# Four seven-product pairs instead of three in each feed-forward stage, and the first weight sum made by an accumulating DMA

## The chip, the cores and the metric

The kernel runs on one core of a Trainium2 chip. The metric is the device time of one launch in microseconds (us). Before the change the median of three runs is 1888.43 us (1888.31 to 1888.49).

## The reference

x is 256 tokens by 1024, float32. Four layers; each is a half-step SwiGLU feed-forward, an attention (stick-breaking, differential, forgetting, stick-breaking), and another half-step feed-forward, all on RMS-normed input with residual adds; a last RMS norm ends it. So there are eight feed-forward stages, and the change is in these alone:

```python
D_MODEL, SEQ, DEPTH, D_FF = 1024, 256, 4, 2816
def swiglu(x, w_gate, w_up, w_down):
    return (jax.nn.silu(x @ w_gate) * (x @ w_up)) @ w_down
for i in range(DEPTH):
    x = x + 0.5 * swiglu(rms_norm(x, norm_g[i, 0]), ffn_w_gate[i, 0], ffn_w_up[i, 0], ffn_w_down[i, 0])
    ...                       # attention of the layer, residual add
    x = x + 0.5 * swiglu(rms_norm(x, norm_g[i, 2]), ffn_w_gate[i, 1], ffn_w_up[i, 1], ffn_w_down[i, 1])
return rms_norm(x, final_g)
```

## The kernel before

**Products.** A float32 product is made of three TensorE matmuls. Each operand is split into a high part (`_hi`, a rounded copy) and a low part (`_lo`, the rest); `product()` (L1272 to L1274) issues hi·hi, hi·lo and lo·hi.

**Chunks.** Weights arrive as one stream of chunks, each 128 partitions by 2048 float32 (1 MB). SP issues the loads in the order of `LOADS`, into 4 places of `raw` (and 2 of `extra`). In the order of `USES`, ScalarE (ACT) makes `w_hi` (`hi`, L465), VectorE (DVE) makes `w_lo` (`lo`, L765), TensorE (PE) uses both. `w_hi` and `w_lo` are rings of 6 chunks: ACT may make chunk c once PE is done with chunk c-6. `split_to(c)` means: make all chunks up to c.

**A feed-forward stage** has 11 units of 256 hidden columns. A plain unit takes a `top` and a `bottom` chunk (gate and up weights of 256 columns side by side, 512 of the 1024 inputs each), with 24 matmuls of 512 columns for each (2 token blocks x 4 slices x 3), and a `down` chunk (24 matmuls). Hidden values are turned by 4 transposes, then split as `m_hi` (ACT, L488) and `m_lo` (DVE, L829).

**Seven-product pairs.** Units (2,3), (5,6) and (8,9), listed by `SEVEN`, are done in pairs: with two token blocks and two halves of the inputs, the 2x2 block product is made with seven block products instead of eight (the scheme of Strassen and Winograd). The parts are `b11, t1, t2, b21, t3, t4, b22`, each a chunk of its own and 12 matmuls (`quarter`). The four loaded chunks are b11, b12, b21, b22; the parts t1, t3, t2, t4 are sums of weight chunks that DVE makes (`form`, L778 to L789) in place, t1 and t4 in a buffer `SUMS` (the first place of `extra`). Sums of tokens are made once a stage. The products gather in PSUM banks; ACT copies partial results out, DVE adds them (L918), ACT applies silu, DVE multiplies by the up part (gates).

**What sets the order.** It is written by hand: `FFN_ORDER` gives the order of chunks for all engines, and each engine's function (`plain_step`, `pair_step`) puts its other work between them. Each engine works strictly in this order and waits on semaphores. GpSimd (POOL) only makes `r_col`, the factor 1/rms of each token (L435, L436).

Of the kernel before, what the change touches and what calls it, by code (L numbers as in the profile page):

```python
# [14 lines left out]
P = 128  # L15
# [8 lines left out]
SEVEN = 2, 5, 8  # L24
# [12 lines left out]
CONSTS = 6  # L37
IDLE_TURNS = 20
IDLE_BETWEEN = 8
RAW = 4  # L40
DMA_SCRATCH = 8192
# [23 lines left out]
FORMS = "t1", "t3", "t2", "t4"  # L65
PARTS = "b11", "t1", "t2", "b21", "t3", "t4", "b22"
PAIR_ORDER = *PARTS[:5], "down", *PARTS[5:]


def ffn_order():  # L70
    order = []
    for s in range(UNITS):
        if s in SEVEN:
            order += [(what, s - (what == "down")) for what in PAIR_ORDER]
# [6 lines left out]
    return order + [("down", UNITS - 1)]  # L81
# [43 lines left out]
def plan():  # L125
# [4 lines left out]
    for layer, n, c0, att, no in phases():  # L130
        order = ATT_ORDER if att else FFN_ORDER
        for w, (what, j) in enumerate(order, c0):
            p = no * len(SEVEN) + SEVEN.index(j) if what in PARTS else None
            if what in ("t1", "t4"):
                uses.append((what, no, j, SUMS, None))
            elif what == "t2":
                uses.append((what, no, j, *places["b11"]))
            elif what == "b22":
                uses.append((what, no, j, EXTRA, p + 1))
            elif what == "t3":  # L140
                uses.append((what, no, j, *places["b12"]))
            else:
                uses.append((what, no, j, len(users) % RAW, len(users) // RAW + 1))
            for load in ("b12",) if what == "t1" else () if what in FORMS or what == "b22" else (what,):
# [3 lines left out]
                users.append(("form", len(FORMS) * (p + 1)) if load in ("b11", "b21") else  # L148
                             ("lo", c0 + order.index(("t3", j)) + 1) if load == "b12" else ("lo", w + 1))
            if what == "t1":  # L150
                earlier = SEVEN.index(j) - 1
                loads.append(("b22", layer, n % 3, j, EXTRA,
                              ("top", no * len(PLAIN) + 1) if earlier < 0 else
                              ("lo", c0 + order.index(("b22", SEVEN[earlier])) + 1)))
    return uses, loads


USES, LOADS = plan()


def trunk(nc, stream, x_in, gains, consts, lam_in, subln_in, wf_in, bf_in, final_in, out):
    with ExitStack() as ctx:
# [13 lines left out]
        extra = sb("extra", [P, 2, CHUNK])  # L176

# [24 lines left out]
        final_gain = sb("final_gain", [P, D])  # L202
        mean = sb("mean", [P, TB])
        r_col = sb("r_col", [P, TB])
        half_neg = sb("half_neg", [P, TB])
        mean_apart = sb("mean_apart", [P, TB])
# [36 lines left out]
        b22_loaded, form_ready = sem("b22_loaded"), sem("form_ready")  # L243
        token_sums_ready, token_hi_ready, token_lo_ready = (
# [54 lines left out]
        first_part, second_part, first_sum = (scratch[:, i, 0:2 * T] for i in range(3))  # L299
        h_first, h_sb = ([scratch[:, i, tb * COLS:(tb + 1) * COLS] for tb in range(TB)] for i in (0, 3))  # L300
# [55 lines left out]

        def unit_bank(s, tb):
            return work[:, (TB if s == 1 else 0) + tb, :]

        def hidden_bank(s):  # L360
            return work[:, 1 if s == 0 else 3 if s - 1 in SEVEN else 2, :]

        def hidden_source(s):
            return h_first if s == 0 else h_sb
# [4 lines left out]
        def slot_free(eng, c):  # L369
# [14 lines left out]
            elif what in PARTS:  # L384
                eng.wait_ge(part_psum, (no * len(SEVEN) + SEVEN.index(j)) * len(PARTS) + PARTS.index(what) + 1)
# [10 lines left out]
        def _(sp):  # L396
            def load(i):
                place, free = LOADS[i][4:]
                if free is not None:
                    sp.wait_ge({"lo": lo_ready, "form": form_ready, "top": top_used}[free[0]], free[1])  # L400
                sp.dma_start(raw_at(place), stream[i]).then_inc(b22_loaded if place == EXTRA else raw_loaded[place], 16)
# [1390 lines left out]
```

## Time and profile before

| | |
|---|---|
| median of 3 runs | 1888.43 us |
| the profiled execution: time, span | 1888.84 us, 1887.0 us |
| PE busy | 1873.5 us, 99% |
| DVE busy | 1519.5 us, 81% |
| ACT busy | 1072.5 us, 57% |
| POOL busy | 19.9 us, 1% |
| DMA | 350.13 MB, mean 186 GB/s |

The span runs from the first to the last instruction; 1.84 us of the execution lie around it. Matmuls are pipelined, so the mean of one (some 390 ns) is longer than the distance from one start to the next, and PE busy is not PE at its peak. The same holds, less, for DVE and ACT.

### The profile page before, as it was taken

The page shows a single profiled execution, that of the slowest core. Times are in us where ns is not written, and L with a number is a line of the kernel's source. Part 1 is how long each engine was busy: PE and PEld are TensorE (multiplying, and loading weights), DVE is VectorE, ACT ScalarE, POOL GpSimd, SP SyncE. Part 2 cuts the span into 40 slices and gives each one's busy share as a digit, 9 for nine tenths or more (in the row PEclk, how much of TensorE's full clock was granted, in tenths as well). Part 3 has the DMA queues.
Part 4 walks back from the last instruction along what each step waited for, and adds up shares of the span by engine and source line. Part 5 has one row for each costly group of instructions (what it writes and reads, how often), then busy time and mean ns, then how long its engine had stood idle before and what let it go on. Part 6 is the DMA issues. An engine that isn't in the chain of part 4 may idle for free.

```text
span 1887.0 us, 22407 instructions
## 1 busy us (share of the span) xinstructions
PE 1873.5 (99%) x9364; PEld 1585.5 (84%) x9364; DVE 1519.5 (81%) x1287; ACT 1072.5 (57%) x1108; POOL 19.9 (1%) x34
## 2 busy tenths in 40 slices
PE   9999999999999999999999999999999999999998
PEld 8888998888888899788888888988888888998886
DVE  7987568987898778898789875689879886569985
ACT  6655455655565544565556554465556654556653
POOL 0000000000000000100000000000000000000000
PEclk9999999999999999999999999999999999999999
DMA  6456343556254643444625454434563544533542
GB/s 249 201 231 262 139 157 134 201 201 238 99 224 195 248 157 112 156 201 200 250 102 227 196 229 157 176 115 201 201 268 125 224 198 189 183 130 136 228 197 86
DMA packets 50052, 350.13 MB, mean 186 GB/s; under 512 B 6168, under 2 KB 6432, under 8 KB 7968
## 3 DMA queue, kind: packets, MB, share of 16 engines
q1 hardware_dynamic: 49360, 346.54, 47.1%
q10 hardware_dynamic: 592, 2.17, 0.4%
q8 instruction: 74, 1.21, 0.2%
q14 instruction: 26, 0.21, 0.0%
HBM read 347.63 MB, written 1.06 MB: 185 GB/s over the span
## 4 chain that ended last, share of the span: by engine, by line
PE 89%; DVE 7%; ACT 2%; issue 1%; DMA 0%; POOL 0%; POOLq 0%; ACTq 0%; DVEq 0%
PE work L1272 18%; PE work L1274 18%; PE work L1273 18%; PE acc L1272 10%; PE acc L1274 10%; PE acc L1273 10%; DVE w_lo L765 3%; PE work L1430 1%; PE acc L1316 1%; PE work L1474 1%; PE work L1608 1%; ACT w_hi L465 1%; PE work L1574 0%; DMA x<-x_dram 0%; PE work L1578 0%
## 5 line engine op out<-in xcount | busy, mean ns | idle before, releaser
L765 DVE TENSOR_TENSOR w_lo<-raw,w_hi 128x2048 fp32r<-128x2048 f32 x327 | 741.3, 2283 | 33.5 <-ACT w_hi L465 33.4
L465 ACT ACTIVATE w_hi<-raw 128x2048 fp32r<-128x2048 f32 x327 | 613.9, 1908 | 83.7 <-DVE raw L785 60.9
L1272 PE MATMUL work<-w_hi,xg 128*128 128x512 f32 x1040 | 409.6, 394 | 1.0 <-DVE xg L1197 1.0
L1274 PE MATMUL work<-w_hi,xg 128*128 128x512 f32 x1040 | 405.5, 390 | 0.0
L1273 PE MATMUL work<-w_lo,xg 128*128 128x512 f32 x1040 | 405.0, 389 | 0.0
L1272 PE MATMUL acc<-w_hi,m_hi 128*128 128x512 f32 x824 | 325.5, 395 | 0.2
L1274 PE MATMUL acc<-w_hi,m_lo 128*128 128x512 f32 x824 | 321.2, 390 | 0.0
L1273 PE MATMUL acc<-w_lo,m_hi 128*128 128x512 f32 x824 | 320.7, 389 | 0.0
L1274 PEld LDWEIGHTS work<-w_hi,xg 128*128 128x128 f32 x1040 | 195.2, 188 | 41.1
L1272 PEld LDWEIGHTS work<-w_hi,xg 128*128 128x128 f32 x1040 | 195.3, 188 | 40.5 <-issue 1.2
L1273 PEld LDWEIGHTS work<-w_lo,xg 128*128 128x128 f32 x1040 | 195.5, 188 | 38.8
L765 DVE TENSOR_TENSOR w_lo<-extra,w_hi 128x2048 fp32r<-128x2048 f32 x72 | 164.4, 2283 | 34.2 <-ACT w_hi L465 34.2
L1274 PEld LDWEIGHTS acc<-w_hi,m_lo 128*128 128x128 f32 x824 | 154.7, 188 | 32.7
L1272 PEld LDWEIGHTS acc<-w_hi,m_hi 128*128 128x128 f32 x824 | 154.8, 188 | 31.6 <-DVE w_lo L765 1.0
L1273 PEld LDWEIGHTS acc<-w_lo,m_hi 128*128 128x128 f32 x824 | 154.9, 188 | 30.7
L465 ACT ACTIVATE w_hi<-extra 128x2048 fp32r<-128x2048 f32 x72 | 135.2, 1912 | 46.1 <-DVE extra L778 36.7
L1274 PE MATMUL work<-w_hi,wide_r 128*128 128x512 f32 x384 | 149.7, 390 | 0.0
L1272 PE MATMUL work<-xg,w_hi 128*128 128x256 f32 x512 | 148.7, 290 | 0.2
L1273 PE MATMUL work<-xg,w_hi 128*128 128x256 f32 x512 | 144.7, 283 | 0.0
L1274 PE MATMUL work<-xg,w_lo 128*128 128x256 f32 x512 | 144.7, 283 | 0.0
L488 ACT ACTIVATE m_hi<-work 128x512 fp32r<-128x512 f32 x88 | 49.8, 594 | 141.1 <-PE work L1430 114.5
L829 DVE TENSOR_TENSOR m_lo<-work,m_hi 128x512 fp32r<-128x512 f32 x88 | 58.4, 686 | 71.6 <-ACT m_hi L488 71.5
(203 smaller groups left out, 2151.8 us busy)
## 6 DMA issues: line engine op xcount, KB each, us to landing
raw<-stream_dram SPq DMA_DIRECT2D x303, 1024.0 KB, 5.1
extra<-stream_dram SPq DMA_DIRECT2D x24, 1024.0 KB, 7.0
x<-x_dram SPq DMA_DIRECT2D x2, 512.0 KB, 8.4
raw<-stream_dram ACTq DMA_DIRECT2D x2, 512.0 KB, 7.9
scratch<-cum_rows ACTq DMA_DIRECT2D x1, 1024.0 KB, 6.5
cst<-consts_dram SPq DMA_DIRECT2D x1, 832.0 KB, 6.5
out_dram<-x SPq DMA_DIRECT2D x3, 256.0 KB, 2.4
final_gain<-final_gain_dram SPq DMA_DIRECT2D x1, 512.0 KB, 6.4
```

What stands on the lines that cost most here:

```text
L465: nc.scalar.activation(w_hi[:, c % RING, :], raw_at(place), ACT.Copy).then_inc(hi_ready, 1)
L488: nc.scalar.activation(m_hi[:, u % 2 * 2:u % 2 * 2 + 2, :], halves(hidden_bank(s)), ACT.Copy).then_inc(h_hi_ready, 1)
L765: nc.vector.tensor_tensor(w_lo[:, c % RING, :], raw_at(place), w_hi[:, c % RING, :].bitcast(F32), ALU.subtract).then_inc(lo_ready, 1)
L829: nc.vector.tensor_tensor(m_lo[:, u % 2 * 2:u % 2 * 2 + 2, :], halves(hidden_bank(s)), m_hi[:, u % 2 * 2:u % 2 * 2 + 2, :].bitcast(F32), A ...
L1272: nc.tensor.matmul(dst, a_hi, b_hi, start=start, stop=False, skip_group_check=skip)
L1273: nc.tensor.matmul(dst, a_hi, b_lo, start=False, stop=False, skip_group_check=skip)
L1274: return nc.tensor.matmul(dst, a_lo, b_hi, start=False, stop=stop, skip_group_check=skip)
L1316: ins = nc.tensor.transpose(turned(bank)[:, d, :], x_part(bank)[:, d * P:(d + 1) * P], ident)
L1430: ins = nc.tensor.transpose(hidden_bank(s)[:, t * T + tb * P:t * T + (tb + 1) * P], h[:, t * P:(t + 1) * P], ident)
L1474: ins = nc.tensor.transpose(hidden_bank(s)[:, t * T + tb * P:t * T + (tb + 1) * P], hidden_source(s)[tb][:, t * P:(t + 1) * P], ident)
L1608: nc.tensor.matmul(bank, v[:, 0, cols], w[:, 0:T], start=True, stop=True)
```

## The change

1. `SEVEN` becomes `2, 4, 7, 9`: four pairs a stage instead of three. Pairs 4 and 9 come straight behind a pair (`chained`); plain are only units 0, 1 and 6. The last unit, 10, is now half of a pair.
2. t1 is no longer made by DVE. The chunk b11 is loaded a second time, into `SUMS`, and then GpSimd issues a DMA that adds b12 to it from DRAM (`accum_op=ALU.add`). For this the signs change: all weight sums are now plain additions, the token sums S1, S2, S4 have other signs, and two of the four results come out negated, which the factor `r_neg` (-r_col, made by GpSimd) takes up. t4 is now formed in b21's place.
3. In a chained pair the order of parts is another (`pair_order`): b22's product, the fourth sum's of the tokens, goes ahead, and the down projection of the unit before is done in halves (single banks in the last pair), between quarters.
4. `raw` has 5 places instead of 4; `final_gain` lies in `extra` and is loaded at the end; `DMA_SCRATCH` is 4096 instead of 8192.

```diff
-SEVEN = 2, 5, 8
+SEVEN = 2, 4, 7, 9
-RAW = 4
-DMA_SCRATCH = 8192
+RAW = 5
+DMA_SCRATCH = 4096
-FORMS = "t1", "t3", "t2", "t4"
+FORMS = "t3", "t2", "t4"
+def pair_order(s):
+    if chained(s):
+        return [("b11", s), ("t1", s), ("b21", s), ("down", s - 2), ("b22", s), ("t2", s),
+                ("down", s - 1), ("t3", s), ("t4", s)]
+    return [("b11", s), ("t1", s), ("t2", s), ("b21", s), ("t3", s), ("down", s - 1), ("t4", s), ("b22", s)]
...
+            if what == "down" and chained(j + 2):
+                loads.append(("b22", layer, n % 3, j + 2, EXTRA, ("lo", c0 + order.index(("b22", j)) + 1)))
+            if what == "down" and j + 1 in SEVEN[:-1]:
+                loads.append(("b11", layer, n % 3, following(j + 1), SUMS, ("lo", c0 + order.index(("t1", j + 1)) + 1)))
...
+            def first_weight_sums(no):
+                for p in range(no * len(SEVEN), (no + 1) * len(SEVEN)):
+                    pool.wait_ge(sums_loaded, 16 * (p + 1))
+                    pool.dma_start(raw_at(SUMS), stream[ADD_FROM[p]], accum_op=ALU.add).then_inc(t1_added, 16)
...
+                if n % 3 != 1:
+                    pool.wait_ge(r_col_ready, n + 1)
+                    nc.gpsimd.tensor_tensor(r_neg[:], r_col[:], minus[:], ALU.mult).then_inc(r_neg_ready, 1)
+                    first_weight_sums(n // 3 * 2 + n % 3 // 2)
...
-                if what in FORMS:
+                if what == "t1":
+                    act.wait_ge(t1_added, 16 * count)
+                elif what in FORMS:
...
+                    def second_of_chain():
+                        split_to(q + 4)
+                        hidden_lo(s - 1)
+                        gate_11()
+                        split_to(q + 5)
+                        form("t4", q)
+                        split_to(q + 7)
+                        sum_12()
+                        split_to(q + 8)
+                        gate_12()
+                        sum_22()
+                        gate_22()
+                        split_to(q + 9)
+                        gate_21()
+                        split_to(q + 10)
+                        if s == UNITS - 2:
+                            hidden_lo(s)
+                            hidden_lo(s + 1)
...
+                    if chained(s):
...
+                        quarter(chain, block_of(0, 0), at["b11"], True, False)
+                        pair_hidden(s - 2)
...
+                        quarter(3, sum_of(S1), at["t1"], True, False)
...
+                        quarter(seed, block_of(0, 1), at["b21"], False, True)
...
+                        pair_hidden(s - 1)
+                        unit_down(s - 2).then_inc(down_used, 1)
...
+                        quarter(3, sum_of(S4), at["b22"], False, True)
+                        quarter(chain, sum_of(S2), at["t2"], False, False)
+                        before, between = ((0, 1), (2, 3)) if s < UNITS - 2 else ((0,), (1,))
+                        unit_down(s - 1, before)
...
+                        quarter(chain, sum_of(S3), at["t3"], False, False)
+                        ins = unit_down(s - 1, between)
...
+                        quarter(chain, block_of(1, 1), at["t4"], False, True)
+                        if s == UNITS - 2:
+                            unit_down(s - 1, (2,))
+                            pair_hidden(s)
+                            unit_down(s - 1, (3,)).then_inc(down_used, 1)
+                            pair_hidden(s + 1)
+                            unit_down(s).then_inc(down_used, 1)
```

How instructions move, on three places. On VectorE, in the second half of a pair: before, from the gate of the first block (L927) on; L918 is a sum of partial results, L765 a `w_lo`, L869 and L935 gates, L778 the next pair's t1, L829 an `m_lo`.

```order
L927 SCALAR_TENSOR_TENSOR scratch<-work,r_col,scratch 128x256 [waits pair_silu_ready]
L918 TENSOR_TENSOR scratch<-work,scratch 128x512 [waits part_psum,part_copied]
L765 TENSOR_TENSOR w_lo<-extra,w_hi 128x2048 [waits hi_ready]
L765 TENSOR_TENSOR w_lo<-raw,w_hi 128x2048 [waits hi_ready]
L869 SCALAR_TENSOR_TENSOR scratch<-scratch,r_col 128x256 [waits pair_silu_ready]
L765 TENSOR_TENSOR w_lo<-raw,w_hi 128x2048 [waits hi_ready]
L935 SCALAR_TENSOR_TENSOR pair_h<-work,r_col,pair_h 128x256 [waits pair_silu_ready]
L765 TENSOR_TENSOR w_lo<-raw,w_hi 128x2048 [waits hi_ready]
L918 TENSOR_TENSOR scratch<-work,scratch 128x512 [waits part_psum,part_copied]
L765 TENSOR_TENSOR w_lo<-raw,w_hi 128x2048 [waits hi_ready]
L869 SCALAR_TENSOR_TENSOR scratch<-scratch,r_col 128x256 [waits pair_silu_ready]
L778 TENSOR_TENSOR extra<-raw 128x2048 [waits raw_loaded2]
```

And in the changed kernel, the first pair of a chain from its first sum (L1011) to the `w_lo` of `down` of its first unit (L865 is `w_lo`, L877 and L881 form t3 and t2 of the next pair, L1034, L1021 and L1027 are gates, L1005 the other sum, L925 is `m_lo`):

```order
L1011 TENSOR_TENSOR scratch<-work,scratch 128x512 [waits part_psum,part_copied]
L865 TENSOR_TENSOR w_lo<-extra,w_hi 128x2048 [waits hi_ready]
L865 TENSOR_TENSOR w_lo<-raw,w_hi 128x2048 [waits hi_ready]
L1034 SCALAR_TENSOR_TENSOR scratch<-scratch,r_neg 128x256 [waits pair_silu_ready]
L865 TENSOR_TENSOR w_lo<-extra,w_hi 128x2048 [waits hi_ready]
L877 TENSOR_TENSOR raw<-extra,raw 128x2048 [waits b22_loaded,raw_loaded0]
L1021 SCALAR_TENSOR_TENSOR pair_h<-work,r_col,pair_h 128x256 [waits pair_silu_ready]
L1005 TENSOR_TENSOR scratch<-work,scratch 128x512 [waits part_psum,part_copied]
L865 TENSOR_TENSOR w_lo<-raw,w_hi 128x2048 [waits hi_ready]
L881 TENSOR_TENSOR raw<-raw 128x2048 [waits lo_ready,form_ready]
L1027 SCALAR_TENSOR_TENSOR scratch<-scratch,r_neg 128x256 [waits pair_silu_ready]
L925 TENSOR_TENSOR m_lo<-work,m_hi 128x512 [waits h_hi_ready]
```

The forms of the next pair, which stood in the plain unit between two pairs, now stand inside the pair. The end of a stage on VectorE, before (unit 10 plain) and then changed (unit 10 in a pair); L1185 and L1324 are the first updates of x:

```order
L829 TENSOR_TENSOR m_lo<-work,m_hi 128x512 [waits h_hi_ready] x2
L863 SCALAR_TENSOR_TENSOR scratch<-work,r_col,scratch 128x256 [waits silu_ready] x2
L765 TENSOR_TENSOR w_lo<-raw,w_hi 128x2048 [waits hi_ready] x2
L829 TENSOR_TENSOR m_lo<-work,m_hi 128x512 [waits h_hi_ready]
L765 TENSOR_TENSOR w_lo<-raw,w_hi 128x2048 [waits hi_ready]
L1185 SCALAR_TENSOR_TENSOR x<-acc,x 128x512 [waits acc_ready] x2
```

```order
L865 TENSOR_TENSOR w_lo<-raw,w_hi 128x2048 [waits hi_ready]
L1021 SCALAR_TENSOR_TENSOR pair_h<-work,r_col,pair_h 128x256 [waits pair_silu_ready]
L865 TENSOR_TENSOR w_lo<-raw,w_hi 128x2048 [waits hi_ready]
L925 TENSOR_TENSOR m_lo<-work,m_hi 128x512 [waits h_hi_ready] x2
L865 TENSOR_TENSOR w_lo<-raw,w_hi 128x2048 [waits hi_ready] x2
L1324 SCALAR_TENSOR_TENSOR x<-acc,x 128x512 [waits acc_ready] x2
```

The last gate (L1021), the `w_lo` of the last down chunk and both last `m_lo` now follow each other directly. On GpSimd, the work of one feed-forward stage in the changed kernel (before, only its first two rows):

```order
L497 TENSOR_TENSOR r_col<-mean,half_neg 128x1 [waits mean_ready]
L498 TENSOR_TENSOR r_col<-mean,half_neg 128x1
L506 TENSOR_TENSOR r_neg<-r_col,minus 128x2 [waits r_col_ready]
L493 DMA extra<-stream_dram 128x2048 [waits sums_loaded] x4
```

Over the program PE has 6720 matmuls of 512 columns instead of 6816; DVE 519 instructions on 2048 columns instead of 495 and 16 more on 512; ACT 423 instead of 399 and 24 more on 512; SP issues 359 chunk loads instead of 327, and GpSimd 32 accumulating ones.

## Rows read from the trace of the kernel before

**Rows 1.** The page: span, busy times, the chain by engine.
```profile
span 1887.0 us, 22407 instructions
...
PE 1873.5 (99%) x9364; PEld 1585.5 (84%) x9364; DVE 1519.5 (81%) x1287; ACT 1072.5 (57%) x1108; POOL 19.9 (1%) x34
...
PE 89%; DVE 7%; ACT 2%; issue 1%; DMA 0%; POOL 0%; POOLq 0%; ACTq 0%; DVEq 0%
```

**Rows 2.** Busy time by stretch: three feed-forward stages (first, fourth, sixth), one attention.
```profile
20.00:198.00 178.00, 177.26 (x808) 146.07 (x808) 154.20 (x116) 108.27 (x103) 1.47 (x2) 1.00 0.54 215
485.60:663.10 177.50, 177.50 (x814) 147.19 (x813) 150.05 (x113) 104.51 (x101) 1.07 (x2) 1.00 0.50 196
1244.20:1422.70 178.50, 178.50 (x818) 148.03 (x817) 154.19 (x115) 107.91 (x103) 1.11 (x3) 1.00 0.50 198
198.00:307.20 109.20, 109.08 (x698) 99.23 (x697) 67.54 (x67) 56.75 (x64) 1.06 (x2) 1.00 0.41 149
```

**Rows 3.** PE in order of time (start, length): two matmuls, 30 apart.
```profile
306.17 0.39 PE L1273 MATMUL work<-w_lo,xg 128*128 128x512 f32 x1
...
312.97 0.39 PE L1273 MATMUL work<-w_lo,xg 128*128 128x512 f32 x1
```

**Rows 4.** PE in order of time: transposes of units 0 and 1, fourth stage.
```profile
495.91 0.60 PE L1474 MATMUL work<-cst,scratch 128*128 128x128 f32 x4
...
509.98 0.60 PE L1474 MATMUL work<-cst,scratch 128*128 128x128 f32 x4
```

**Rows 5.** Groups by line (busy us, mean ns, idle before): splits and one form.
```profile
L765 DVE TENSOR_TENSOR w_lo<-raw,w_hi 128x2048 fp32r<-128x2048 f32 x327 | 741.3, 2283 | 33.5 <-ACT w_hi L465 33.4
L465 ACT ACTIVATE w_hi<-raw 128x2048 fp32r<-128x2048 f32 x327 | 613.9, 1908 | 83.7 <-DVE raw L785 60.9 <-DMA raw<-stream_dram 22.7
...
L781 DVE TENSOR_TENSOR raw<-extra,raw 128x2048 f32<-128x2048 f32 x24 | 54.8, 2282 | 0.0
```

**Rows 6.** DVE in order of time, first pair of the fourth stage.
```profile
517.96 2.28 DVE L765 TENSOR_TENSOR w_lo<-raw,w_hi 128x2048 fp32r<-128x2048 f32 x1
520.16 0.68 DVE L859 TENSOR_TENSOR wide_r<-wide,wide_r 128x512 fp32r<-128x512 f32 x1
...
522.96 0.47 DVE L927 SCALAR_TENSOR_TENSOR scratch<-work,r_col,scratch 128x256 f32<-128x256 f32 x1
523.36 0.68 DVE L918 TENSOR_TENSOR scratch<-work,scratch 128x512 f32<-128x512 f32 x1
523.96 2.28 DVE L765 TENSOR_TENSOR w_lo<-extra,w_hi 128x2048 fp32r<-128x2048 f32 x1
```

**Rows 7.** DVE in order of time, start of the fourth stage.
```profile
486.60 2.29 DVE L765 TENSOR_TENSOR w_lo<-raw,w_hi 128x2048 fp32r<-128x2048 f32 x1 [1.04 <-ACT w_hi L465]
...
491.18 0.48 DVE L863 SCALAR_TENSOR_TENSOR scratch<-work,r_col,scratch 128x256 f32<-128x256 f32 x1 [1.89 <-ACT scratch L499]
```

**Rows 8.** DMA from issue to landing, us: loads into extra, then into raw.
```profile
DMA to landing us min/median/max: 4.7/7.0/8.5
...
DMA to landing us min/median/max: 4.6/5.1/14.6
```

**Rows 9.** ACT in order of time: `m_hi`, a silu.
```profile
511.62 0.58 ACT L488 ACTIVATE m_hi<-work 128x512 fp32r<-128x512 f32 x1
...
529.71 0.47 ACT L560 ACTIVATE pair_h<-work,r_col 128x256 f32<-128x256 f32 x1 [0.52 <-PE work L1274]
```

**Rows 10.** Busy time by stretch: DMA in a pair.
```profile
525.00:535.00 10.00, 10.00 (x46) 8.29 (x45) 10.00 (x8) 7.17 (x7) 0.00 (x0) 1.00 0.96 373
```

**Rows 11.** ACT in order of time: `w_hi` of unit 1, first stage.
```profile
19.37 3.71 ACT L465 ACTIVATE w_hi<-raw 128x2048 fp32r<-128x2048 f32 x2
```

**Rows 12.** POOL and DVE in order of time, around two r_col.
```profile
777.68 2.53 POOL L435 TENSOR_TENSOR r_col<-mean,half_neg 128x1 f32<-128x1 f32 x1 [14.93 <-DVE mean L811]
...
955.29 0.55 POOL L435 TENSOR_TENSOR r_col<-mean,half_neg 128x1 f32<-128x1 f32 x1 [172.87 <-DVE mean L811]
...
777.52 4.49 DVE L765 TENSOR_TENSOR w_lo<-raw,w_hi 128x2048 fp32r<-128x2048 f32 x2
```

More of the change, by code:

```diff
@@ L63, with chained, following, part_count @@
              + [("o", PAIRS - 2), ("o", PAIRS - 1)])
-FORMS = "t1", "t3", "t2", "t4"
+FORMS = "t3", "t2", "t4"
 PARTS = "b11", "t1", "t2", "b21", "t3", "t4", "b22"
-PAIR_ORDER = *PARTS[:5], "down", *PARTS[5:]
+def chained(s):
+    return s in SEVEN and s - 2 in SEVEN
+def pair_order(s):
[3 more added lines that the diff above has]
+    return [("b11", s), ("t1", s), ("t2", s), ("b21", s), ("t3", s), ("down", s - 1), ("t4", s), ("b22", s)]
+def following(s):
+    return SEVEN[SEVEN.index(s) + 1]
+def part_count(s, what):
+    return [part for part, unit in pair_order(s) if unit == s].index(what) + 1
+def block_count(s, which):
+    return (("c11", "c12", "c22", "c21") if chained(s) else ("c11", "c22", "c21", "c12")).index(which) + 1
+def sum_count(s, which):
+    return (("c12", "c22") if chained(s) else ("c22", "c12")).index(which) + 1
 def ffn_order():
@@ L73, in ffn_order @@
         if s in SEVEN:
-            order += [(what, s - (what == "down")) for what in PAIR_ORDER]
+            order += pair_order(s)
         elif s - 1 in SEVEN:
@@ L80, in ffn_order @@
             order += [("top", s), ("bottom", s)] + [("down", s - 1)] * (s > 0)
-    return order + [("down", UNITS - 1)]
+    return order + [("down", UNITS - 2), ("down", UNITS - 1)]
 FFN_ORDER = ffn_order()
@@ L147, in plan @@
                 loads.append((load, layer, n % 3, j, r % RAW, users[r - RAW] if r >= RAW else None))
-                users.append(("form", len(FORMS) * (p + 1)) if load in ("b11", "b21") else
+                users.append(("form", len(FORMS) * (p + 1)) if load == "b11" else
+                             ("lo", c0 + order.index(("t4", j)) + 1) if load == "b21" else
                              ("lo", c0 + order.index(("t3", j)) + 1) if load == "b12" else ("lo", w + 1))
[L150 to L154, printed above, removed]
+            if n % 3 and layer < DEPTH - 1 and what == "down" and j in (UNITS - 3, UNITS - 2):
+                load, place, last = ("b11", SUMS, "t1") if j == UNITS - 3 else ("b22", EXTRA, "b22")
+                loads.append((load, layer + 1, 0, SEVEN[0], place, ("lo", c0 + order.index((last, SEVEN[-1])) + 1)))
+            if what == "down" and chained(j + 2):
+                loads.append(("b22", layer, n % 3, j + 2, EXTRA, ("lo", c0 + order.index(("b22", j)) + 1)))
+            if what == "down" and j + 1 in SEVEN[:-1]:
+                loads.append(("b11", layer, n % 3, following(j + 1), SUMS, ("lo", c0 + order.index(("t1", j + 1)) + 1)))
+            if what == "t4" and j in SEVEN[:-1] and not chained(following(j)):
+                loads.append(("b22", layer, n % 3, following(j), EXTRA, ("lo", c0 + order.index(("b22", j)) + 1)))
     return uses, loads
 USES, LOADS = plan()
+ADD_FROM = [i for i, load in enumerate(LOADS) if load[0] == "b12"]
+LAST_SUM = [c for c, use in enumerate(USES) if use[0] == "t1"][-1]
 def trunk(nc, stream, x_in, gains, consts, lam_in, subln_in, wf_in, bf_in, final_in, out):
@@ L942, in ffn @@
+                    (second_of_chain if chained(s) else first_of_chain)()
                 for s in range(UNITS):
@@ L1405, in pair_step @@
                     if s - 1 > 1:
                         pe.wait_ge(h_ready, (f * len(PLAIN) + PLAIN.index(s - 1)) * TB + 2)
-                    quarter(1, block_of(0, 0), q, True, False)
+                    quarter(chain, block_of(0, 0), at["b11"], True, False)
                     hidden(s - 1)
```

329 lines of the change are left out of this document (203 added, 126 removed).

## The prediction

> **What bounds the kernel now.** I read the page first: PE is busy 99% of the span and is 89% of the chain that ended last, so whatever PE doesn't have to do is gained, as long as the other engines keep up [rows 1]. Then the busy times by stretch. A feed-forward stage is 177.5 us, with no moment in which PE is idle; DVE is busy 150.1 to 154.2 us of it, ACT 104.5 to 108.3 us, and an attention leaves DVE 41.7 us free [rows 2]. Since a busy PE may hide waits inside its overlapping matmuls, I read their distance in order of time: 30 matmuls on, the start is 6.80 us later, 0.2267 us for each [rows 3]. Between the transposes of units 0 and 1 lie 60 matmuls (bottom of unit 1, down of unit 0, b11) and 14.07 us; 60 x 0.2267 = 13.60, so four transposes cost 0.47 us [rows 4]. A stage has 492 gate and up and 264 down matmuls: 756 x 0.2267 = 171.4 us. The 6.1 us that are left are 15 groups of four transposes (11 of hidden values, 4 of x), 0.41 each. So PE doesn't wait in a stage, and its work can be priced by its count. The clock is granted in full throughout (the 1.00 in rows 2).
>
> **What the change removes.** Each further pair saves one of eight block products, 12 matmuls: 8 pairs x 12 = 96, 96 x 0.2267 = 21.8 us. A stage becomes 174.8 us of PE work. Everything else must be hidden under it.
>
> **What it adds on DVE and ACT.** The instructions are as long as 2.28 us (DVE) and 1.91 us (ACT) on a chunk [rows 5], but on DVE they start 2.20 us apart; 512 columns cost 0.60 and 256 columns 0.40 [rows 6]. DVE gets 24 instructions on a chunk (3 more `w_lo` a stage; the forms stay 12, since four pairs make 3 each where three made 4) and 16 sums: 24 x 2.20 + 16 x 0.60 = 62.4 us, 7.8 a stage. That is 157.9 to 162.0 of 174.8 us, 90 to 93%. It fits in the mean, but what was 23 to 27 us of free time a stage is now 13 to 17, so I followed the places where DVE waits for PE and PE then waits for DVE. ACT gets 24 chunks at 1.82 (two in 3.71 in rows 11, less their overlap) and 24 copies at 0.5 = 56 us, 7 a stage: 115 of 174.8 us, no bound.
>
> **The tight cycle: from a pair's third sum to the down product of a chained pair** (twice a stage). From the end of t3's product PE has down, t4, b22, then b11, t1, b21 of the next pair: 84 matmuls and two groups of transposes, 84 x 0.2267 + 0.94 = 20.0 us. In that time DVE, which can't start before it, has a sum, seven instructions on a chunk (`w_lo` of b22, b11, t1; form t3; `w_lo` b21; form t2; `w_lo` of down), three gates, another sum and an `m_lo`: 0.1 + 7 x 2.20 + 3 x 0.40 + 3 x 0.60 = 18.5 us. Its second sum needs b22's product, at 10.9 us, and DVE would be there at 10.3: 0.7 us more with the hand-over, 19.2 in all. Margin: 0.8 us. Here form t3 also needs the next b22 in `extra`, whose load is released by the `w_lo` of the present b22, at 2.9 us, and DVE wants it at 7.7. A load lands 5.1 us after issue in the middle for raw, and 7.0 for extra [rows 8]. With 5.1 it is 0.3 us late, which the wait of 0.7 takes up: no cost. With 7.0 it is 2.2 late, less 0.6 and 0.8: 0.8 us of stall. I take 5.1: before, the load into extra is one of a run of loads, while here it is issued alone, more than 3 us behind the one before it. Fewer than 3 us are needed for 1 MB when the queues are full, at 373 GB/s [rows 10]. So 0, with the bounds 0 and 16 x 2.3 = 36 us (landing after 8.5 us).
>
> **The rest of a chained pair.** PE has 96 matmuls from the start of that down to the end of t4, 21.8 us; DVE has seven instructions on a chunk, an `m_lo`, three gates and two sums, 18.4 us. It waits for t2's and t3's products on the way (about 2 us by the same counting), and `w_lo` of the next top is there 1.4 us early. No cost. Were the down projection not in halves between t2, t3 and t4, DVE's sums would have 2.7 us less each; that is what the moved instructions pay for.
>
> **The first pair of a stage.** Before, `w_lo` of down 1 ends at 520.16, and PE, which turns unit 1 at 509.98 [rows 4] and then has 48 matmuls, asks for it at 521.3: 1.2 us of margin [rows 6]. DVE loses a form (2.20) ahead of this. It gains one `w_lo` at the start of the stage, because one chunk fewer is made ahead, but there it waited 1.04 and 1.89 us anyway [rows 7]. The margin grows, to as much as 3.4 us. No cost.
>
> **The end of a stage.** Unit 10 was plain, with its hidden values ready long before its down product. Now, from the end of t4's product, ACT makes a silu (0.47), DVE the gate (0.40), then `w_lo` of down 10 (2.20), then `m_lo` of unit 9 (0.60): 4.0 us with hand-overs. PE has two banks of down 8 (12 matmuls, 2.7 us) and two groups of transposes, 3.66 us. `m_hi` [rows 9] fits beside. PE waits 0.35 us, 8 times: 2.8 us, between 0 and 8 (if the hand-overs are twice as long).
>
> **The start.** Two chunks, 2.1 MB, are now loaded ahead of unit 1's: 5.6 us later at the rate of rows 10. ACT took that unit's chunk at 19.37 without waiting [rows 11]. In return DVE makes no t1 there. I take 1.0 us, between 0 and 3.
>
> **Edits at no cost.** SP's three loads behind the wait for the last `pv` of an attention: the down 0 chunk is wanted some 22 us after the stage begins. `r_neg`, 0.55 us on idle POOL, is first used 30 us on. `q0` is no longer split ahead of an attention, and its `w_lo` delays the mean by 2.2 us; PE has 48 matmuls (10.9 us) before it asks for the factors. One more place in raw only brings loads forward. The traffic grows by 64 MB of reads (32 second b11, 32 added b12), and the accumulating ones read their destination too: from half of the 16 engines' time to about two thirds.
>
> **The accumulating DMA.** The trace has none. Its window: b11 may be reloaded when `w_lo` of the pair's t1 is done, and the next t1 is wanted by ACT 19.7 us later in a chain (eight DVE instructions on a chunk, 17.6, with 3.4 of small ones and 1 of waits, less 2.3 for ACT's own). The reload takes 5.1 of it; 14.6 are left. From below, it takes as long as the fastest plain load, 4.6 us [rows 8]; with the destination read as well, 2 x 2.8 + 2.3 = 7.9; from above, at a quarter of the rate, 4 x 2.8 + 2.3 = 13.5 or more. I take 8 to 10, so it is hidden. POOL has nothing else to do then; only `r_col` of the next stage stands behind it.
>
> A row speaks against this: POOL's r_col took 2.53 us when two `w_lo` stood on DVE at 777.52, against 0.55 otherwise [rows 12]. The Trainium skill (SBUF — State Buffer, Who interferes with whom) says that a DVE instruction with two SBUF inputs contends with a GpSimd instruction that reads SBUF, and the trace agrees, 2.53 to 0.55. The same section infers that descriptor generation needs only the write side and isn't held up by tensor_tensor; by that, each accumulating DMA would start at once. By the lock it would wait for one or more `w_lo`, and that is rival C.
>
> **The sum.** The profiled execution took 1888.84 us, 0.4 above the median: 1888.84 - 21.8 + 2.8 + 1.0 = 1870.8, less 0.4 = 1870.4 us.
>
> **Rivals.**
> A, the forecast: 1866 to 1876 us.
> B, DVE's cycle between pairs becomes the bound: the load of b22 takes as long as loads into extra did. For it: the median of 7.0, and DVE full for 10 us on end in a pair (the 10.00 in rows 10). Against it: the load is issued alone. At 7.0: 16 x 0.8 = 13 us, 1883. At 8.5: 36 us, 1906. It turns to slower at a landing of 7.4 us (18 / 16 = 1.1 of stall).
> C, slower: the accumulating DMA is later than its window, because POOL's descriptors wait behind DVE's `w_lo`, or the adding is slow. Place: ACT's t1 in the chained pairs, and all of ACT's work behind it. With 18 us: 3.4 x 16 = 54, 1925 us. It turns to slower at 14.6 + 1.1 = 15.7 us. For it: rows 12, and a `w_lo` or form on DVE nearly all the time. Against it: three waits of 2.2 us on top of 8 still fit (14.6).
> That the matmuls don't go is excluded: PE's list has 96 fewer.
>
> **Chances.** A 0.60; B 0.25 (0.16 of it faster, 0.05 within, 0.04 slower); C 0.11, slower; anything else 0.04. About 0.2%, 3.8 us, is what a measurement of this kernel can tell from no change. Faster: 0.60 + 0.16 + 0.02 = 0.78; within: 0.06; slower: 0.04 + 0.11 + 0.01 = 0.16. The range goes from 1865 (A with no stall is 1866.6) to 1888, which takes in A and most of B, 0.8; C and the far end of B are outside. A alone: 1866 to 1876.
>
> **What would show it.** PE: a stage of 174.8 to 175.5 us, and 0.2267 between matmuls as before. DVE: 158 to 162 us busy a stage; no wait of PE for `w_lo` above a few us in all; if B holds, waits of L877 (form t3) for a DMA and of PE's down product for `w_lo`. The landing of extra's loads near 5 us. ACT's `w_hi` from extra should not wait for the accumulating DMA; if C holds, it does, by several us each time. At each stage's end PE waits 0.3 to 0.4 us for `m_lo`. I am wrong if PE has idle time in the chained pairs above 0.3 us each.

## The result, and the profile after

The changed kernel takes 1896.14 us (median of 6 runs, 1894.38 to 1897.77), the kernel before 1888.46 (1888.31 to 1889.57): ratio 1.0040, 95% interval 1.0030 to 1.0051. It is slower by 7.7 us, where 18 us less were forecast. The profiled execution took 1896.24 us.

The page after, the same lines as [rows 1]:
```profile
span 1894.2 us, 22684 instructions
...
PE 1860.1 (98%) x9268; PEld 1566.5 (83%) x9268; DVE 1584.0 (84%) x1327; ACT 1133.2 (60%) x1156; POOL 66.3 (3%) x75
...
PE 75%; DVE 16%; DMA 4%; ACT 2%; issue 2%; POOL 0%; POOLq 0%; DVEq 0%; ACTq 0%
```
PE lost its 96 matmuls and 13 us of busy time, and the span grew all the same. In the chain that ended last, DVE more than doubled (7 to 16%) and DMA came up from 0 to 4%. So PE now waits. ("Fourth stage" counts the attention too, here as in the text before: it is the third of the eight feed-forward stages.) Busy time of two stages (length; busy PE, PEld, DVE, ACT, POOL; granted clock; DMA share; GB/s), to hold against [rows 2]:
```profile
484.90:662.80 177.90, 176.50 (x805) 145.49 (x804) 160.02 (x120) 112.45 (x107) 8.39 (x7) 1.00 0.67 230
1422.00:1600.70 178.70, 176.58 (x805) 145.50 (x804) 160.08 (x120) 112.01 (x107) 8.40 (x7) 1.00 0.67 231
```
From one stage's first transposes of x to the next, five of the six middle feed-forward stages last 177.9 to 178.9 us and the one from 770 us on 181.2; before it was 178.4 to 178.5 and 180.5. DVE's 160 us and the DMA share of 0.67 are what was forecast. Matmuls still start 0.2267 us apart. Whatever lies between two starts above that is a stall, and read so the places are few and mostly the same (a time is the start of the matmul before the wait):

| PE waits for | where | us each | sum |
|---|---|---|---|
| `w_lo` of the down product | first chained pair of a stage, 8 times | 0.84 to 1.66 | 10.9 |
| `m_lo` of unit 9 | end of a stage, 8 times | 0.59 | 4.7 |
| the gate of c21 | first chained pair, at 73.50 and 829.74; end of a stage, once | 1.98, 2.38, 0.53 | 4.9 |
| the sum of c22, ahead of t4's product | pair 9, 8 times | 0.53 | 4.2 |
| `w_lo` of unit 1, `m_lo` of unit 0 | first stage | 2.82, 1.25 | 4.1 |
| (slow clock behind the first of these) | first stage | | 1.7 |

That is 30.5 us. The 96 matmuls would have brought 1888.84 to 1867.0, and 1896.24 is 29.2 above it. The kernel before had two stalls of its own that are gone after, 0.9 us in the first stage (at 44.58) and 1.6 here:
```profile
801.02 0.47 PE L1272 MATMUL work<-w_hi,scratch_r 128*128 128x512 f32 x1 [1.35 <-DVE w_lo L765]
```
x landed some 0.6 us sooner too, so 27.4 of the 30.5 us are new. The other 1.8 lie in gaps too short for the table, some 0.2 us a stage, and 0.2 outside the span. PE in order of time at one of the first kind, fourth stage:
```profile
547.18 0.60 PE L1606 MATMUL work<-cst,scratch 128*128 128x128 f32 x4
548.46 0.50 PE L1413 MATMUL acc<-w_hi,m_hi 128*128 128x512 f32 x1 [0.68 <-DVE w_lo L865]
```
From four transposes to the next matmul it is 0.36 us when nothing waits; here 1.28, a stall of 0.92. DVE ahead of it, same stage:
```profile
527.94 0.69 DVE L1011 TENSOR_TENSOR scratch<-work,scratch 128x512 f32<-128x512 f32 x1 [0.21 <-PE work L1415]
528.55 2.28 DVE L865 TENSOR_TENSOR w_lo<-extra,w_hi 128x2048 fp32r<-128x2048 f32 x1
...
533.35 2.28 DVE L865 TENSOR_TENSOR w_lo<-extra,w_hi 128x2048 fp32r<-128x2048 f32 x1
537.53 2.29 DVE L877 TENSOR_TENSOR raw<-extra,raw 128x2048 f32<-128x2048 f32 x1 [1.90 <-DMA extra<-stream_dram]
...
546.13 2.28 DVE L865 TENSOR_TENSOR w_lo<-raw,w_hi 128x2048 fp32r<-128x2048 f32 x1
```
and SP's load of that b22, released by the `w_lo` of 528.55:
```profile
530.86 0.33 SPq L452 DMA_DIRECT2D extra<-stream_dram  x1
```
The load lands 6.6 us after issue, form t3 (L877) is kept for 1.90 us, and PE loses 0.92: a margin of 1.0. At 1296.71, in another stage, DVE waited 2.73 us and PE lost 1.65, a margin of 1.1. In the second chain of the fourth stage the same load was issued at 610.29, landed after 4.7 us, and form t3 started at 615.13 without a wait. What the DMA engines had in hand differs:
```profile
529.00:534.00 5.00, 5.00 (x23) 4.13 (x22) 5.00 (x4) 3.91 (x3) 0.00 (x0) 1.00 0.99 377
...
608.00:611.00 3.00, 3.00 (x15) 2.47 (x14) 3.00 (x3) 2.83 (x3) 0.00 (x0) 1.00 0.63 257
```
In the first chain they are full, from 514 us on:
```profile
514.00:529.00 15.00, 15.00 (x69) 12.40 (x68) 14.79 (x11) 11.57 (x11) 0.86 (x1) 1.00 0.98 307
```
An accumulating DMA issued at 517.32 is among what they move there. Whether it is the cause, these rows alone don't tell.

### The profile page after: what moved, and what is told of

It is laid out like the page before. It is cut to its first block, busy times and chain, and to the rows that moved or that the text cites. A ratio compares the mean times of both kernels' runs of the same rounds, so it can differ in the third digit from the quotient of the medians.

```text
span 1894.2 us, 22684 instructions
## 1 busy us (share of the span) xinstructions
PE 1860.1 (98%) x9268; PEld 1566.5 (83%) x9268; DVE 1584.0 (84%) x1327; ACT 1133.2 (60%) x1156; POOL 66.3 (3%) x75
## 4 chain that ended last, share of the span: by engine, by line
PE 75%; DVE 16%; DMA 4%; ACT 2%; issue 2%; POOL 0%; POOLq 0%; DVEq 0%; ACTq 0%
PE work L1413 15%; PE work L1415 15%; PE work L1414 15%; DVE w_lo L865 8%; PE acc L1413 8%; PE acc L1415 8%; PE acc L1414 8%; DMA extra<-stream_dram 3%; DMA raw<-stream_dram 1%; ACT w_hi L533 1%; DVE raw L881 1%; PE acc L1457 1%; DVE m_lo L925 1%; PE work L1606 1%; DVE raw L877 1%
## 5 line engine op out<-in xcount | busy, mean ns | idle before, releaser
L865 DVE TENSOR_TENSOR w_lo<-raw,w_hi 128x2048 fp32r<-128x2048 f32 x359 | 813.0, 2283 | 46.9 <-ACT w_hi L533 46.8
L533 ACT ACTIVATE w_hi<-raw 128x2048 fp32r<-128x2048 f32 x359 | 675.4, 1909 | 78.7 <-DVE raw L881 57.1
L1413 PE MATMUL work<-w_hi,xg 128*128 128x512 f32 x880 | 347.6, 395 | 6.7 <-DVE scratch L1011 3.0
L1415 PE MATMUL work<-w_hi,xg 128*128 128x512 f32 x880 | 343.9, 391 | 0.0
L1414 PE MATMUL work<-w_lo,xg 128*128 128x512 f32 x880 | 343.2, 390 | 0.0
L1413 PEld LDWEIGHTS work<-w_hi,xg 128*128 128x128 f32 x880 | 165.6, 188 | 43.9 <-DVE scratch L1011 6.4
L1415 PE MATMUL work<-w_hi,wide_r 128*128 128x512 f32 x512 | 199.5, 390 | 0.0
L1415 PEld LDWEIGHTS work<-w_hi,xg 128*128 128x128 f32 x880 | 165.4, 188 | 35.1
L1414 PEld LDWEIGHTS work<-w_lo,xg 128*128 128x128 f32 x880 | 165.8, 188 | 32.9
L865 DVE TENSOR_TENSOR w_lo<-extra,w_hi 128x2048 fp32r<-128x2048 f32 x64 | 146.1, 2282 | 0.0
L1415 PEld LDWEIGHTS work<-w_hi,wide_r 128*128 128x128 f32 x512 | 96.1, 188 | 20.5
L1413 PE MATMUL work<-w_hi,scratch_r 128*128 128x512 f32 x256 | 102.9, 402 | 0.0
```

Of the source, the lines that this page charges most:

```text
L533: nc.scalar.activation(w_hi[:, c % RING, :], raw_at(place), ACT.Copy).then_inc(hi_ready, 1)
L865: nc.vector.tensor_tensor(w_lo[:, c % RING, :], raw_at(place), w_hi[:, c % RING, :].bitcast(F32), ALU.subtract).then_inc(lo_ready, 1)
L1413: nc.tensor.matmul(dst, a_hi, b_hi, start=start, stop=False, skip_group_check=skip)
L1414: nc.tensor.matmul(dst, a_hi, b_lo, start=False, stop=False, skip_group_check=skip)
L1415: return nc.tensor.matmul(dst, a_lo, b_hi, start=False, stop=stop, skip_group_check=skip)
```

## The experiments

All are compared with runs of the kernel before on the same chip, whose median was 1888.5 to 1888.8 each time; the changed kernel's 1896.1 is the other reference.

**The start: the loads behind unit 1.**
```
-            if (what, j) == ("top", 1) and n == 0:
+            if (what, j) == ("down", 0) and n == 0:
```


> The changed kernel with one edit: the first stage loads the second b11 and b22 of the first pair ahead of the down 0 chunk instead of ahead of unit 1. Theory (the lost time is a sum of small stalls, one of them at the start): the wait of 2.82 us at 22.94 goes, the granted clock stays at 1.00 around 24 to 30 us, and the waits of 1.25 and 1.98 us behind it shrink; 5 to 7 us less than 1896.1, so 1889 to 1891. Rival (the memory traffic or DVE as a whole is too much, and the first stage is only where it shows): the stalls move on by some us and the time stays above 1894.


Measured: 1893.4 us (1891.0 to 1898.7), ratio 1.0025 (1.0015 to 1.0035). The wait at 22.94 is gone, and in its place PE stands 5.47 us at 34.34, once, for `m_lo` behind a `w_lo` whose chunk is late. So the stall was moved, and little of it removed: the theory's mechanism holds only for the order of the waits, its size missed (1889 to 1891), and the rival's 1894 was missed too. That the start is bound by the bytes is a reading here; `e6_first_sum_by_dve` tests it.

**Form t3 behind the sum of c12.**
```
                         split_to(q + 9)
-                        form("t3", q + 8)
                         gate_21()
                         sum_12()
+                        form("t3", q + 8)
```


> The changed kernel with one edit: in the first pair of a chain DVE makes form t3 of the next pair behind the gate of c21 and the sum of c12 instead of ahead of them; nothing is left out. Theory (DVE stands still for the load of b22, and PE's down product of the chained pair is late by that): DVE's waits of L877 for the DMA, 18.9 us in ten places, all but go, PE's stalls ahead of that down product (0.9 to 1.75 us a stage) fall to below 0.3, 8 to 11 us less: 1885 to 1888. Rival (DVE's cycle is full, the load only stands where DVE would have waited for the product of b22 anyway): the wait turns up ahead of the sum of c12 instead, PE's stall stays, 1894 to 1897.


Measured: 1912.5 us (1911.6 to 1912.9), ratio 1.0125 (1.0108 to 1.0142). The waits of L877 fell to 1.2 us as expected, and it is 16 us slower: the theory's cure was wrong. DVE in order of time:
```profile
540.42 0.48 DVE L1021 SCALAR_TENSOR_TENSOR pair_h<-work,r_col,pair_h 128x256 f32<-128x256 f32 x1 [0.91 <-ACT pair_h L615]
542.70 0.69 DVE L1005 TENSOR_TENSOR scratch<-work,scratch 128x512 f32<-128x512 f32 x1 [1.80 <-PE work L1415]
543.31 2.28 DVE L877 TENSOR_TENSOR raw<-extra,raw 128x2048 f32<-128x2048 f32 x1
```
Form t3 had filled the time in which DVE must wait for b22's product. Now it waits 0.91 and 1.80 us there, and PE stalls 1.8 us at the down product of all 16 chained pairs, 29 us in all. This cycle has one place where a wait is free, and the form stood in it.

**DVE's order at the end of a chain.**
```
+                        sum_22()
                         gate_12()
-                        sum_22()
...
                         gate_21()
+                        if s == UNITS - 2:
+                            hidden_lo(s)
                         split_to(q + 10)
                         if s == UNITS - 2:
-                            hidden_lo(s)
                             hidden_lo(s + 1)
```


> The changed kernel with one edit, in DVE's list of a chained pair: the sum of c22 goes ahead of the gate of c12, and at the end of a stage m_lo of unit 9 goes ahead of w_lo of down 10. Theory: PE's waits of 0.53 us ahead of t4's product of pair 9 and of 0.69 us ahead of down 9, eight times each (9.8 us), fall to 0.1 and 0.2: 7 us less, 1889. Rival (ACT's silu and hand-overs set the end, not DVE's order): the waits stay at two thirds or more and the time above 1893.


Measured: 1887.3 us (1884.8 to 1890.0), ratio 0.9993 (0.9983 to 1.0002), 8.8 us less than the changed kernel. Both kinds of stall are gone in all eight stages. DVE in the changed kernel near 470 us, then here:
```profile
469.52 0.48 DVE L1021 SCALAR_TENSOR_TENSOR pair_h<-work,r_col,pair_h 128x256 f32<-128x256 f32 x1 [0.85 <-ACT pair_h L615]
469.93 2.28 DVE L865 TENSOR_TENSOR w_lo<-raw,w_hi 128x2048 fp32r<-128x2048 f32 x1
472.12 0.68 DVE L925 TENSOR_TENSOR m_lo<-work,m_hi 128x512 fp32r<-128x512 f32 x1
```
```profile
469.45 0.48 DVE L1021 SCALAR_TENSOR_TENSOR pair_h<-work,r_col,pair_h 128x256 f32<-128x256 f32 x1 [0.29 <-ACT pair_h L615]
471.38 0.69 DVE L925 TENSOR_TENSOR m_lo<-work,m_hi 128x512 fp32r<-128x512 f32 x1 [1.45 <-ACT m_hi L556]
471.99 2.28 DVE L865 TENSOR_TENSOR w_lo<-raw,w_hi 128x2048 fp32r<-128x2048 f32 x1
```
`m_lo` had stood behind a `w_lo` that PE wants 5 us later. The edit also moves the sum of c22 in pair 9, and both belong to the 8.8 us: 4.7 and 4.2 in the table.

**No adding at all**, and **a plain load in its place**: two kernels that tell what it is in the accumulating DMA that costs.
```
-                    act.wait_ge(t1_added, 16 * count)
+                    act.wait_ge(sums_loaded, 16 * count)
...
-                    first_weight_sums(n // 3 * 2 + n % 3 // 2)
```


> The changed kernel without the accumulating DMA: t1's product is made from b11 alone (b12 isn't added to it), so the 32 transfers on POOL's queue and their 64 MB of reads and added reads go; all else stays. Theory (b22 is issued too late for any landing above 5 us, and the accumulating DMA isn't what costs): loads still land after 5.5 us or more, the stalls at the down product of the first chained pair, at t4 of pair 9 and at the end stay, 1892 to 1896. Rival (the adding traffic slows the plain loads from 5.1 to 6.9 us and by that makes all the waits for b22): raw lands after 5.1 us again, the waits of L877 fall from 18.9 to below 5 us, the start is as before, 1885 or less.


```
-                    pool.dma_start(raw_at(SUMS), stream[ADD_FROM[p]], accum_op=ALU.add).then_inc(t1_added, 16)
+                    pool.dma_start(raw_at(SUMS), stream[ADD_FROM[p]]).then_inc(t1_added, 16)
```


> The changed kernel with POOL's DMA as a plain load of b12 over b11, without adding (t1's product is then that of b12): the same issue, the same bytes from DRAM, no read of the destination. Theory (what the accumulating DMA costs is its share of the 16 DMA engines while these are full): it lands sooner, after 5 to 6 us instead of 8.2, raw's loads after 6 to 6.5 instead of 6.9, and the time lies between e4_no_adding and the changed kernel, 1886 to 1891. Rival 1 (only the bytes read count): 1894 to 1897. Rival 2 (only the adding counts): as e4_no_adding, 1882 to 1885.


Measured: 1883.2 us (1880.2 to 1885.6), ratio 0.9971 (0.9959 to 0.9982) without, and 1882.2 (1881.0 to 1884.3), 0.9965 (0.9952 to 0.9978), with the plain load. My theory missed in both: the first went by its rival (1885 or less), the second by rival 2 (only the adding counts). Without the transfer the waits of L877 fall from 18.9 to 1.9 us, PE's stalls at the down product from 10.9 to 1.7, in one place; with the plain load they are 3.4 and 3.8. And the plain load, with the same 1 MB from DRAM, the same issue on POOL and the same queue, costs no time over leaving it out. The adding does. Of the 14.0 us between the changed kernel and the plain load, 7.1 lie at the down products, 4.9 at the gates of c21, which no longer keep PE waiting, and 1.3 at the start.

The landing of b22 in the first chain shows it: 6.5 to 7.4 us in the changed kernel's eight stages, 4.7 to 5.1 with the plain load in seven of them (6.5 in one). Yet the DMA engines are nearly as full there. The five us behind the issue of the same load (526.26, landed after 5.1 us), to hold against the row of 529.00:
```profile
526.00:531.00 5.00, 5.00 (x23) 4.13 (x22) 5.00 (x4) 2.25 (x2) 0.00 (x0) 1.00 0.95 354
```
So a share near 1 at the issue doesn't make a landing late by itself; the 15 us ahead of it were at 0.88 here and at 0.98 in the changed kernel. The median landing in raw hardly tells either: 6.9 us in the changed kernel, 6.6 with the plain load, 5.9 without.

DMA by queue (packets, MB, share of the 16 engines' time) and POOL's DMA (KB, us to landing), first the changed kernel, then the plain load:
```profile
q0 software_dynamic: 4608, 33.56, 9.4%
...
extra<-stream_dram POOLq DMA_DIRECT2D x32, 1024.0 KB, 8.2
```
```profile
q0 software_dynamic: 4608, 33.56, 4.7%
...
extra<-stream_dram POOLq DMA_DIRECT2D x32, 1024.0 KB, 5.1
```
The same bytes take the engines twice the time when they are added, 5.6 us of all 16 for each MB (9.4% of 1894 / 32) against 2.8. Where the engines are full, as in the first chain, other loads are pushed back by that.

**`w_lo` of b22 ahead of the sum of c22.**
```
                         gate_11()
-                        sum_22()
                         split_to(q + 7)
+                        sum_22()
```


> The changed kernel with one edit: in the first pair of a chain DVE makes w_lo of b22 ahead of the sum of c22, not behind it, so that the next b22 is asked for earlier and the work moves out of the tight cycle. Theory (the landing of b22, issued when the 16 DMA engines are full, is late by 0.9 to 1.8 us more than PE's margin of 0.9): the load is issued 1.3 us (first chain) and 2.5 us (second) earlier, DVE's waits of L877 for it fall from 18.9 to under 8 us, PE's stalls at the first chained down product from 11 to under 3 us: 1886 to 1889. Rival (the transfer starts when the queue ahead of it is done, whenever it is issued): it lands at the same time as before, the waits stay near 18 us and so does the time, 1894 to 1897.


Measured: 1887.4 us (1886.0 to 1889.0), ratio 0.9992 (0.9983 to 1.0002), 8.8 us less. DVE, fourth stage, to hold against the rows at 527.94 and 537.53:
```profile
526.06 2.28 DVE L865 TENSOR_TENSOR w_lo<-extra,w_hi 128x2048 fp32r<-128x2048 f32 x1
528.26 0.68 DVE L1011 TENSOR_TENSOR scratch<-work,scratch 128x512 f32<-128x512 f32 x1
...
535.07 2.29 DVE L877 TENSOR_TENSOR raw<-extra,raw 128x2048 f32<-128x2048 f32 x1 [1.33 <-DMA extra<-stream_dram]
```
The load is issued at 528.37 and lands 6.6 us later, as before, so issuing earlier lands it earlier and the rival falls. The gain of the issue is 0.9 us here, less than the 1.3 I expected. DVE's waits for b22 didn't fall, they rose to 24.1 us in 16 places, because DVE is ahead of its work; PE's stalls at the down product fell from 10.9 to 3.5. A DVE wait by itself says nothing here; its margin to PE does.

**The first pair's first sum by DVE.** In the first stage alone, DVE adds b11 and b12, and b22 is loaded behind unit 1:
```
+                    if n == 0 and s == 1:
...
+                        nc.vector.tensor_tensor(raw_at(SUMS), raw_at(b11[3]), raw_at(b12[3]),
+                                                ALU.add).then_inc(t1_made, 1)
...
-                for p in range(no * len(SEVEN), (no + 1) * len(SEVEN)):
+                for p in range(max(no * len(SEVEN), 1), (no + 1) * len(SEVEN)):
```


> The changed kernel with the first pair of the first stage alone treated as in the kernel before: DVE adds b11 and b12 itself, so one load of b11 and one accumulating DMA (2.1 MB) go from the start, and b22 is loaded behind unit 1. Theory (the start is bound by what the DMA engines move: the wait of 5.5 us that only changed its place in e1_start is 2.1 MB at 373 GB/s, 5.6 us): the stalls of the first stage ahead of its chained pair fall from about 5.5 us to below 1.5, 4 to 6 us less than 1896.1, so 1890 to 1892. Rival (DVE's order is at fault there): 1893 or more, as DVE has an instruction more.


Measured: 1889.6 us (1885.7 to 1893.8), ratio 1.0006 (0.9996 to 1.0015), 6.6 us less. Before the first chained pair PE now waits once, 1.28 us at 42.87; the stalls in that pair stay (2.42 and 1.67). Taking the bytes, and the adding, away did more than moving them.

**All three together.**


> The edits of e3_end, e5_lo_first and e6_first_sum_by_dve in one kernel, nothing left out. Theory (the stalls are separate and add up: 8.8 us measured in e3_end, 8 to 10 and 4 to 6 expected of the others): 1896.1 - 22 = 1872 to 1876, faster than both kernels. Rival (they take each other's place, since DMA and DVE stay near full): 1883 to 1888.


Measured: 1874.9 us (1874.1 to 1875.3), ratio 0.9925 (0.9910 to 0.9941): faster than both kernels, as the theory had it (1872 to 1876), and most of what the separate gains add up to (8.8 + 8.8 + 6.6 = 24.2; measured 21.2). The page and one stage:
```profile
PE 82%; DVE 12%; DMA 2%; ACT 2%; issue 2%; POOL 0%; POOLq 0%; DVEq 0%; ACTq 0%
```
```profile
481.00:657.00 176.00, 176.00 (x806) 145.39 (x805) 159.22 (x120) 112.05 (x106) 8.39 (x7) 1.00 0.67 233
```
A stage of 176.0 us with PE busy throughout, and DVE as full as in the changed kernel. Only at 70 to 78 us and at 828 does PE still wait in a chained pair, 2.8 and 1.6 us.

**Four pairs without the accumulating DMA.** c2_all with every t1 made by DVE, ahead of the next `w_lo` of b11:
```
                         sum_22()
+                        first_sum_by_dve(q + 8)
                         split_to(q + 8)
```


> c2_all with every t1 made by DVE (31 more instructions on a chunk, ahead of w_lo of the next b11; no load of b11 into extra, no accumulating DMA): four pairs without the other half of the change. It frees the DMA engines (raw lands after 5 us again, no wait of DVE for b22) and puts 31 x 2.20 = 68 us on DVE, 16 of them in the tight cycle between a third sum and the next down product, where PE's margin was 0.9 us and is up to 2.5 with c2_all's order. Theory (DVE's order between pairs is what binds, more than its sum): stalls of 0.5 to 1.5 us in each of 16 cycles, 1883 to 1899. Rival (the accumulating DMA costs as much as it saves, DVE's free 14 us a stage take the sums): 1873 to 1878.


Measured: 1910.5 us (1909.8 to 1911.5), ratio 1.0116 (1.0099 to 1.0133). The direction was the theory's, the size was beyond it (1883 to 1899): PE stalls 21.1 us in 16 places for the down product's `w_lo` and 12.8 in nine for a gate. Loads into raw land after 5.4 us here. So against DVE's sums in this place of its order the accumulating DMA is worth 35.5 us to the four-pair kernel, in spite of its price; another place for them was not tried.

**The down product whole.** c2_all with this:
```
-                        before, between = ((0, 1), (2, 3)) if s < UNITS - 2 else ((0,), (1,))
+                        before, between = ((0, 1, 2, 3), ()) if s < UNITS - 2 else ((0,), (1,))
```


> c2_all with the down product of pair 4's predecessor unit whole, ahead of t3's product, not in halves: t4's product then stands directly behind t3's, in eight places. Theory (the sum of c22 must read the bank in between: 0.68 us and two hand-overs, where pair 9's one bank of 1.36 us was 0.53 short with a gate ahead of the sum): a stall of 1.2 to 1.5 us in each of the eight, 1883 to 1888. Rival (PE's later work has that much slack to give back): 1875 to 1878.


Measured: 1890.6 us (1889.7 to 1895.1), ratio 1.0013 (1.0004 to 1.0022), 15.7 us more than c2_all. PE waits 1.02 us for the sum of c22 in eight places, a little less than expected, and 0.47 more each time for a later `w_lo`, which was not expected: 11.9 us in all, and the time is above the 1883 to 1888 of the theory. The halves pay 2 us a stage.

## Why the prediction was wrong

- **The removed work**: right. 9268 matmuls, 0.2267 apart, full clock in all stages but the first; c2_all has a stage of 176.0 us, 2.4 under the 178.4 of before, where 2.7 were removed. The stage was said to last 177.5, but that is the length of the window in [rows 2]; from transposes to transposes it is 178.4. The sum takes only the difference and isn't touched. That PE doesn't wait in a stage holds for two of the three windows of [rows 2] and not for all stages: the kernel before lost 0.9 and 1.6 us in two stages.
- **DVE and ACT in the mean**: right, 160 and 112 us a stage (forecast 158 to 162, 115).
- **The tight cycle**: this step failed, in one term. The margin of 0.8 us was about right (1.0). What I called 5.1 us, the landing of the next b22, "because it is issued alone", is 6.5 to 7.4 in the first chain of a stage and 4.7 to 4.8 in the second. Rival B priced it: 0.8 us a pair at 7.0. It happens in 8 places of 16, at 0.84 to 1.66, with two late gates in the same pairs: 15.3 us where 0 was forecast. The reason given against rival B was the wrong question. Issued just as alone, the load lands after 4.7 to 5.1 us in seven of eight stages once POOL's DMA doesn't add. [rows 10] could have warned that the engines are full in that pair (0.96).
- **The accumulating DMA**: its own time was right (8.2; forecast 8 to 10), and it never held up PE, so rival C is out. It wasn't hidden from ACT: in seven first pairs of a stage ACT waited for it, 15.0 us in all, against the sign that ACT wouldn't wait. But I let it end there. Its cost, put at nothing, is the 5.6 us of engine time that it takes from the others' loads: with a plain load instead, the kernel is 14 us faster. The Trainium skill (SBUF — State Buffer, Who interferes with whom) infers that descriptor generation isn't held up by a tensor_tensor on DVE. The trace agrees where it can be read: the DMA issued on POOL at 808.95 lies wholly beside a `w_lo` of DVE, and landed after 7.7 us, as fast as any.
```profile
806.64 4.49 DVE L865 TENSOR_TENSOR w_lo<-raw,w_hi 128x2048 fp32r<-128x2048 f32 x2
808.95 0.86 POOL L493 DMA_DIRECT2D extra<-stream_dram  x1 [19.50 <-DMA extra<-stream_dram]
```
- **The end of a stage**: 0.35 us forecast, 0.59 found, 4.7 us in place of 2.8. I counted the same instructions in the same order, and gave the hand-overs between them too little. The stall of 0.53 ahead of t4's product in pair 9 (4.2 us) I missed: I took the halves as cover enough for both pairs, but pair 9 has one bank there, 1.36 us, against a gate, a sum and hand-overs of 1.9.
- **The start**: 1.0 us forecast, 5.8 found, beyond the upper bound of 3. The 5.6 us of loads were counted rightly and then discounted because ACT hadn't waited [rows 11]; moved behind unit 1 (`e1_start`) they cost about as much, taken away (`e6_first_sum_by_dve`) 6.6 us less. Of the accumulating DMA of that pair I had counted nothing.
- **Edits at no cost**: `r_neg` took some 2.2 us in three stages and 0.2 in five. In those three, at 316.74, 1253.56 and 1719.11, POOL's DMA behind it also landed late, after 10.7 to 11.0 us; the plain load did so too, 7.2 to 7.5 against 5.1. PE lost nothing by it, and why is open. Attention stages are as long as before (108.0 to 110.8 us).
- The statement that I am wrong if PE idles above 0.3 us in the chained pairs was the right test: it loses 1.4 in the mean of eight first chained pairs, 1.9 with the gates.

The sum as it should have been: -21.8 + 15.3 (first chained pairs) + 4.7 + 4.2 + 0.5 (ends) + 5.8 (start) = +8.7. Less 2.5 for the two stalls that the kernel before had and 0.6 for x, and 1.8 more in short gaps, it is +7.4, as far as the two profiled executions are apart. The 1.8 is what is left over, and is not explained one by one.

## What to carry to other kernels

Price a load by where it stands and by what else the change gives the DMA engines around it, not by the median of its kind: the same load landed after 6.6 us beside accumulating transfers and after 5.1 beside plain ones, with a share of 0.95 or more in both. Count an accumulating DMA of this kind twice in the engines' time, and ask whose load that delays. In a cycle between two in-order engines, look for the wait that is free and keep the instruction that may be late in it; and move first what releases a load. When a change adds bytes to a stretch that DMA bounds, moving the loads moved the stall here, and taking them away took it away.

## What the runs showed of the hardware

- An accumulating DMA of 1 MB from DRAM into SBUF lands after 8.2 us in the median, where the plain one on the same queue takes 5.1, and takes twice the engine time (9.4 to 4.7%).
- After a wait of PE of 2.83 us in the first stage the granted clock fell to 0.5, the 1.2 GHz level, for some 3 us, in the changed kernel and in others with such a wait; in e2_form_later, after a wait as long (2.83), it stayed at 2.4 GHz:
```profile
24.00:30.00 6.00, 4.01 (x11) 3.14 (x12) 5.62 (x6) 4.07 (x4) 0.00 (x0) 0.72 1.03 314
```
```profile
24.00:30.00 6.00, 3.83 (x17) 3.18 (x18) 5.64 (x5) 3.90 (x4) 0.00 (x0) 1.00 1.03 318
```
  It cost nothing: with the slow clock the next wait was 1.25 us, without it 2.83, since both waited for the same chunk. Behind that second wait of 2.83 the clock of e2_form_later fell too:
```profile
41.00:46.00 5.00, 5.00 (x16) 3.93 (x16) 4.96 (x3) 0.80 (x2) 0.00 (x0) 0.66 0.00 2
```
  In e3_end it fell after a wait of 2.32 us, in e9_down_whole it didn't after one of 2.60. What decides stays open.
- A POOL instruction of 128x2 (`r_neg`) took 2.2 us in three of eight places and 0.2 in the others.
- The changed kernel and most of its near kin spread over 3 to 8 us from run to run (1891.0 to 1898.7 in e1_start), the kernel before over 1.3 beside the changed one. In e2_form_later it is 1.3 and in c2_all, whose waits mostly don't reach PE, 1.1, both in four runs only. That the landing times make the spread is a guess and not shown.
